# Choosing experts tile by tile and moving the overflow passes to the middle of each expert stage, in a four-layer transformer kernel

## What is computed

```python
lg = xt @ w_rg + b_rg                      # 4 group logits per token
g_sel = argmax(lg); p_grp = max(softmax(lg))
le_sel = (xt @ w_re + b_re).reshape(t, 4, 8)[g_sel]   # the 8 experts of that group
top_l, top_i = top_k(le_sel, 2)
gate = p_grp * softmax(top_l)
y = sum over the two chosen experts e: gate * ((silu(x @ w1[e]) * (x @ w3[e])) @ w2[e])
```

## Time and profile before

| | us |
|---|---|
| runs (3) | 1964.44, 1967.55, 1974.81; median 1967.55 |
| the profiled execution, its own time | 1970.61 |
| its span (first to last instruction) | 1968.9 |
| TensorE busy | 1561.1 (79%) |
| VectorE busy | 417.5 (21%) |
| ScalarE busy | 247.0 (13%) |
| weight queue's packets | 86.5% of 16 DMA engines' span |

### The profile page before, as it was taken

The page is one execution under the profiler, slowest core; times in us unless marked ns, Lnnn a source line. Parts: engine busy times, 40 slices in busy tenths (PEclk is TensorE's granted clock), DMA queues, the critical chain, the costliest instruction groups (busy, mean ns, idle before and its releaser), DMA issues.

```text
span 1968.9 us, 23180 instructions
## 1 busy us (share of the span) xinstructions
PE 1561.1 (79%) x10204; PEld 753.7 (38%) x10204; DVE 417.5 (21%) x900; ACT 247.0 (13%) x527; POOL 86.3 (4%) x140
## 2 busy tenths in 40 slices
PE   8898777899888787989996677776889777667675
PEld 4654433664464344445541222221355222212222
DVE  3341111226331110564410010000043000000001
ACT  1310000136211110156000000000011000000000
POOL 1100000101000000112100000000000000000000
PEclk9999988899899898999997888887899888888888
DMA  7659999669759999389689999999985999999995
GB/s 279 240 198 422 423 422 417 253 236 389 296 235 412 421 420 382 121 314 374 250 329 424 423 425 425 423 423 425 423 350 236 424 423 423 425 424 424 423 422 248
DMA packets 122894, 711.11 MB, mean 361 GB/s; under 512 B 8376, under 2 KB 13480, under 8 KB 49056
## 3 DMA queue, kind: packets, MB, share of 16 engines
q1 hardware_dynamic: 116368, 697.14, 86.5%
q0 software_dynamic: 4320, 9.78, 1.5%
q10 hardware_dynamic: 2096, 2.57, 0.4%
HBM read 708.17 MB, written 1.05 MB: 360 GB/s over the span
## 4 chain that ended last, share of the span: by engine, by line
PE 48%; DMA 39%; DVE 6%; SPq 2%; issue 2%; ACT 2%; POOL 0%; DVEq 0%; PEldq 0%; ACTq 0%; POOLq 0%
DMA ring<-in_moe_w 22%; PE pa L752 7%; PE pb L735 6%; DMA work<-in_moe_w 5%; DMA ring<-in_moe_w_down 5%; PE pa L770 4%; DMA work<-in_moe_w_down 3%; PE acc L814 3%; PE pb L720 3%; PE acc L1304 3%; PE acc L1309 3%; SPq L676 2%; PE acc L1049 2%; PE acc L1223 2%; DMA mod<-in_moe_w 2%
## 5 line engine op out<-in xcount | busy, mean ns | idle before, releaser
L735 PE MATMUL pb<-ring,XT 128*32 128x512 f32 x1488 | 278.9, 709 | 85.8 <-DMA ring<-in_moe_w 77.0
L752 PE MATMUL pa<-ring,work 128*32 128x512 f32 x1056 | 219.9, 754 | 79.1 <-DMA ring<-in_moe_w 46.2
L735 PEld LDWEIGHTS pb<-ring,XT 128*32 128x32 f32 x1488 | 64.6, 126 | 247.8 <-issue 122.5
L770 PE MATMUL pa<-work,HM 128*128 128x128 f32 x1024 | 131.6, 291 | 19.9 <-issue 19.9
L814 PE MATMUL acc<-XT,work 128*128 128x512 f32 x256 | 118.4, 605 | 35.2 <-DVE XT L870 22.4
L770 PEld LDWEIGHTS pa<-work,HM 128*128 128x128 f32 x1024 | 130.2, 207 | 34.8 <-issue 34.8
L860 DVE TENSOR_TENSOR work<-work,pb 128x256 f32<-128x256 f32 (+1 forms) x32 | 17.7, 555 | 574.0 <-PE pb L735 433.9
L735 PE MATMUL pb<-work,XT 128*32 128x512 f32 x480 | 114.5, 708 | 29.1 <-DMA work<-in_moe_w 29.1
L752 PEld LDWEIGHTS pa<-ring,work 128*32 128x32 f32 x1056 | 48.6, 132 | 203.6 <-issue 90.5
L720 PE MATMUL pb<-ring,XT 128*32 128x256 f32 x1728 | 109.8, 380 | 10.6 <-DMA ring<-in_moe_w_up 6.1
L752 PE MATMUL pa<-work 128*32 128x512 f32 x384 | 90.1, 784 | 26.0 <-DMA work<-in_moe_w 15.4
(11 more groups left out here) (403 smaller groups left out, 1741.3 us busy)
## 6 DMA issues: line engine op xcount, KB each, us to landing
ring<-in_moe_w SPq DMA_DIRECT2D x135, 2048.0 KB
work<-in_moe_w SPq DMA_DIRECT2D x46, 2048.0 KB
ring<-in_moe_w_up SPq DMA_DIRECT2D x28, 2048.0 KB
ring<-in_moe_w_gate SPq DMA_DIRECT2D x26, 2048.0 KB
ring<-in_moe_w_down SPq DMA_DIRECT2D x24, 2048.0 KB
ring<-in_w_mod SPq DMA_DIRECT2D x48, 1024.0 KB
mod<-in_moe_w SPq DMA_DIRECT2D x11, 2048.0 KB
work<-in_moe_w_down SPq DMA_DIRECT2D x8, 2048.0 KB
```

What stands on the lines that cost most here:

```text
L735: last = nc.tensor.matmul(hbank[m][j * CAP:(j + 1) * CAP, :], m_xg[:, k, j * CAP:(j + 1) * CAP], slot_of(s0 + j // 2)[:, at:at + fn], star ...
L752: last = nc.tensor.matmul(pa[j * CAP:(j + 1) * CAP, h, :], m_ht[:, c, j * CAP:(j + 1) * CAP], slot_of(i)[:, at:at + 512], start=(c == 0), ...
L770: last = nc.tensor.matmul(xg_ps[:, k, :], HM[:, tt, k * P:(k + 1) * P], m_p[:, tt, :], start=(tt == 0), stop=(tt == TT - 1))
```

## The change

- `PASS_AT = 4`: on all four engines the wait, the register loads and the branch around the overflow passes stand between rounds 3 and 4 and not between 6 and 7. The waits inside the condition are moved with it.
- The logits of tile t go to bank t of `pa`, and `logits_done` is raised once a tile. VectorE runs the choice once for each tile, in 16 operations of half the width; the match against the maximum and the order of the candidates are one operation, with the maximum read per partition. `order` is a new constant made by two operations on GpSimd. Both differences for the exponentials come behind `assign_ready`.
- In expert stages ScalarE copies all four turned halves.
- In the nsa phase 6 idle matmuls stand ahead of the transposes of tile 0 and 10 ahead of those of tile 1.

Context lines are mostly left out:

```diff
@@ -38,6 +38,7 @@
+PASS_AT = ROUNDS // 2
@@ -163,6 +164,7 @@
         iota = sb("iota", [P, CAP])
+        order = sb("order", [P, CAP])
@@ -298,15 +300,17 @@
             for t in range(TT):
+                if ph.kind == "nsa":
+                    warm_tensor(pe, (pa, pb)[t][:, 0, :], (6, 10)[t])
-        def transpose_scalar(act, n, dst):
-            for i in range(3):
+        def transpose_scalar(act, n, dst, parts=3):
+            for i in range(parts):
@@ -563,8 +567,8 @@
                 for k in range(KC):
-                    last = nc.tensor.matmul(pa[:, 0, t * 64:t * 64 + NG + NE], XT[:, k, t * P:(t + 1) * P], wr[:, k, :], start=(k == 0), stop=(k == KC - 1))
-            last.then_inc(logits_done, 1)
+                    last = nc.tensor.matmul(pa[:, t, 0:NG + NE], XT[:, k, t * P:(t + 1) * P], wr[:, k, :], start=(k == 0), stop=(k == KC - 1))
+                last.then_inc(logits_done, 1)
@@ -602,36 +606,37 @@
-            def first_of(out_, x, m, iv, tmp, n):
-                link(v.tensor_tensor(tmp, x, bc(m.unsqueeze(2), [P, TT, n]), ALU.is_equal))
-                link(v.scalar_tensor_tensor(tmp, tmp, -64.0, bc(iv.unsqueeze(1), [P, TT, n]), ALU.mult, ALU.add))
-                link(v.tensor_reduce(m_s[:, 15, :], tmp, AX.X, ALU.min))
-                link(v.tensor_tensor(out_, tmp, bc(m_s[:, 15, :].unsqueeze(2), [P, TT, n]), ALU.is_equal))
-            dve.wait_ge(logits_done, ph.moe + 1)
-            dve.wait_ge(wr_loaded, 96 * (ph.moe + 1))
-            link(v.tensor_tensor(m_log, pa[:, 0, 0:2 * 64].rearrange("p (t n) -> p t n", t=TT)[:, :, 0:NG + NE],
-                                 bc(br[:, :].unsqueeze(1), [P, TT, NG + NE]), ALU.add))
             gmax, l1, l2, dif = (m_s[:, i, :] for i in (0, 1, 2, 4))
-            link(v.tensor_reduce(gmax, lg, AX.X, ALU.max))
-            first_of(m_g[0], lg, gmax, iota[:, 0:NG], m_g[2], NG)
+            lm, o1, o2, tmp = m_t
+            def best(x, top, tmp, t, n):
+                at_ = m_s[:, 15, t:t + 1]
+                link(v.tensor_reduce(top[:, t:t + 1], x, AX.X, ALU.max))
+                link(v.scalar_tensor_tensor(tmp, x, top[:, t:t + 1], order[:, 0:n], ALU.is_equal, ALU.mult))
+                link(v.tensor_reduce(at_, tmp, AX.X, ALU.min))
+                return at_
+            dve.wait_ge(wr_loaded, 96 * (ph.moe + 1))
+            for t in range(TT):
+                dve.wait_ge(logits_done, TT * ph.moe + t + 1)
+                link(v.tensor_tensor(m_log[:, t, :], pa[:, t, 0:NG + NE], br[:, :], ALU.add))
+                g = m_g[2][:, t, :]
+                at_ = best(lg[:, t, :], gmax, g, t, NG)
+                link(v.tensor_scalar(g, g, at_, NEG, ALU.not_equal, ALU.mult))
+                link(v.tensor_tensor(lm[:, t, :].rearrange("p (g e) -> p g e", g=NG), le[:, t, :].rearrange("p (g e) -> p g e", g=NG),
+                                     bc(g.unsqueeze(2), [P, NG, EPG]), ALU.add))
+                at_ = best(lm[:, t, :], l1, tmp[:, t, :], t, NE)
+                link(v.tensor_scalar(o1[:, t, :], tmp[:, t, :], at_, None, ALU.is_equal))
+                link(v.scalar_tensor_tensor(lm[:, t, :], o1[:, t, :], 3 * NEG, lm[:, t, :], ALU.mult, ALU.add))
+                at_ = best(lm[:, t, :], l2, tmp[:, t, :], t, NE)
+                link(v.tensor_scalar(o2[:, t, :], tmp[:, t, :], at_, None, ALU.is_equal))
+                if t == 0:
+                    link(v.tensor_tensor(m_a[:, t, :], o1[:, t, :], o2[:, t, :], ALU.add))
+            v.tensor_tensor(m_a[:, t, :], o1[:, t, :], o2[:, t, :], ALU.add).then_inc(assign_ready, 1)
             v.tensor_tensor(m_g[1], lg, bc(gmax.unsqueeze(2), [P, TT, NG]), ALU.subtract).then_inc(rexp_in, 1)
-            link(v.tensor_scalar(m_g[2], m_g[0], 1.0, -NEG, ALU.subtract, ALU.mult))
-            lm, o1, o2, tmp = m_t
-            link(v.tensor_tensor(lm.rearrange("p t (g e) -> p t g e", g=NG), le.rearrange("p t (g e) -> p t g e", g=NG),
-                                 bc(m_g[2].unsqueeze(3), [P, TT, NG, EPG]), ALU.add))
-            link(v.tensor_reduce(l1, lm, AX.X, ALU.max))
-            first_of(o1, lm, l1, iota[:, 0:NE], tmp, NE)
-            link(v.scalar_tensor_tensor(lm, o1, 3 * NEG, lm, ALU.mult, ALU.add))
-            link(v.tensor_reduce(l2, lm, AX.X, ALU.max))
-            first_of(o2, lm, l2, iota[:, 0:NE], tmp, NE)
             v.tensor_tensor(dif, l2, l1, ALU.subtract).then_inc(rexp_in, 1)
-            v.tensor_tensor(m_a, o1, o2, ALU.add).then_inc(assign_ready, 1)
@@ -872,14 +877,14 @@
             n = moe_slots(ph.fn)
-            for g in range(ROUNDS - 1):
+            for g in range(PASS_AT):
             with sp.If(more > 0):
-                sp.wait_ge(freed, ph.slot0 + (ROUNDS - 1) * n)
+                sp.wait_ge(freed, ph.slot0 + PASS_AT * n)
@@ -890,7 +895,8 @@
             sp.wait_ge(xfreed, (base + more) * (ROUNDS * UNITS) + CREDIT)
-            whole_sync(sp, ph, ROUNDS - 1)
+            for g in range(PASS_AT, ROUNDS):
+                whole_sync(sp, ph, g)
@@ -908,7 +914,7 @@
-                pe.wait_ge(R[0]["y_copied"], 2 * (ROUNDS * (ph.moe + 1) - 1) + START)
+                pe.wait_ge(R[0]["y_copied"], 2 * (ROUNDS * ph.moe + PASS_AT) + START)
@@ -916,7 +922,8 @@
                         round_tensor(pe, ph, R[1], t, wait_full, (xfreed, unit), lambda i: ring[:, i % XSLOTS, :])
-            main_round(ROUNDS - 1)
+            for g in range(PASS_AT, ROUNDS):
+                main_round(g)
@@ -931,15 +938,15 @@
                      lambda e: e.wait_ge(freed, ph.slot0 + g * n + n))
-            for g in range(ROUNDS - 1):
+            for g in range(PASS_AT):
             with eng.If(more > 0):
-                eng.wait_ge(R[0]["added"], ROUNDS * (ph.moe + 1) - 1 + START)
-                eng.wait_ge(R[0]["rank_next"], ROUNDS * (ph.moe + 1) - 1 + START)
+                eng.wait_ge(R[0]["added"], ROUNDS * ph.moe + PASS_AT + START)
+                eng.wait_ge(R[0]["rank_next"], ROUNDS * ph.moe + PASS_AT + START)
@@ -973,6 +981,8 @@
             g.tensor_copy(iota[:, :], iota_i[:, :]).then_inc(consts, 1)
+            link(g.tensor_copy(order[:, :], iota_i[:, :]))
+            link(g.tensor_scalar(order[:, :], order[:, :], 64.0, None, ALU.subtract))
@@ -2361,7 +2371,7 @@
                         by_run_scalar(act, ph, 0)
-                    transpose_scalar(act, ph.xt, XT)
+                    transpose_scalar(act, ph.xt, XT, 4)
@@ -2378,7 +2388,6 @@
                 if ph.kind == "moe":
-                    transpose_vector(dve, ph.xt, XT)
```

## The result

The changed kernel takes 1943.36 us (median of 4 runs, 1941.98 to 1944.58), the kernel before 1966.04 beside it (4 runs, 1964.44 to 1974.81). The ratio is 0.9873, with a 95% interval of 0.9841 to 0.9905: faster by 1.3%, clear of the noise. The forecast was 1951.3 in a range of 1944 to 1961. The direction is right, the gain is larger than forecast, and the median lies just under the range. Profile against profile the gain is 26.0 us (1970.6 to 1944.58), where the sum made 16.3.

A forecast was written before the change was run, and what follows sets the result against it. Weight DMA was taken to bound expert stages, TensorE counting only at their beginnings and ends. 10.4 - 2.2 + 2.4 + 2.7 + 3.0 = 16.3 us off 1970.6 makes 1954.3, as a median 1951.3; range 1944 to 1961.

The forecast's parts named there:

- Stage 2's end: Round 7 of stage 2: without the overflow condition, idle gaps and slow passes go; gain 10.4 us.
- Stage 2's middle: Round 4 of stage 2: the moved stall frees slots late and the weight queue runs dry; cost 2.2 us.
- The other branch that the prediction named: Stage 2, round 4: if the second gap is absent, slots are freed before the queue is dry; cost 0.
- its upper bound of 7: Stage 2, round 4: if the stall is half as long again, 5.2 us more, the cost is about 7.
- Stage 1: Its end gains 2.4 us, then waits for round 7's last weights; the condition in its middle costs 0.
- VectorE's chain: Router, tile 1: 16 operations instead of 22 take 3.85 us; gain 2.7 us over four stages (0 to 4.2).
- The nsa phase's beginning: Idle matmuls keep the clock up for tile 1's transposes and L2116's first passes; gain 3.0 us (0 to 3.4).
- The clock may fall in another place of this stretch; I leave it at 0, with some 3 us either way.: Router: a shift of the clock's slow stretch was counted as 0, with some 3 us either way.
- The fourth copy: Router: ScalarE's copy of the fourth turned half ends when VectorE's did; cost 0, between -0.1 and 0.1 us.
- The stall did not stay at the end: Rival: round 7 is stopped again, only router and nsa gains remain, 5.7 us, 1961.9; chance 0.12.
- the gains were not clipped: Rival: stage 1's data, nsa weights or the router's clock take gains back, leaving 7.3 us, 1960.3; chance 0.14.
- the middle's stall did not empty the queue in any stage: Rival: round 4's stall empties the weight queue in every stage, 10.3 us slower, 1977.9; chance 0.05.

The follow-up runs named there:

- e7: The changed kernel without the overflow passes and their condition on all four engines; 1942.07 us (0.9861).
- e1: The kernel before with only the overflow condition moved between rounds 3 and 4; 1956.04 us (0.9923).
- e10: The kernel before with twelve idle matmuls under TensorE's wait for the first weights, shifting later code; 1965.0 us (0.9977).
- e11: The changed kernel with twelve idle matmuls under TensorE's wait for the first weights, shifting later code; 1945.33 us (0.9885).
- e6: The changed kernel with VectorE copying the fourth turned half again, as before the change; 1956.77 us (0.9958).
- e4: The changed kernel with the overflow condition back before the last round, router and nsa parts kept; 1950.44 us (0.9908).
- e3: The kernel before with only the idle matmuls ahead of the nsa phase's transposes; 1962.44 us (0.9959).
- e8: The kernel before without the overflow passes and their condition on all four engines; 1954.73 us (0.9919).
- e12: The kernel before with 12 instead of 6 idle matmuls ahead of TensorE's router wait in stages 2 and 3; 1959.28 us (0.9956).
- e2: The kernel before with only the router part: choice tile by tile, the constant and ScalarE's fourth copy; 1962.42 us (0.9960).
- e0: The changed kernel a second time, nothing altered; 1943.0 us (0.9867).
- e9: The changed kernel with six additions linked into tile 1's VectorE chain, making it as long as before; 1955.62 us (0.9936).

## Why the prediction was right and wrong

- **Stage 2's end** (-10.4): right, -10.30; the last weights fit, as worked out, and e7 without any condition has -10.34. The "40.3 us after the old L814 began" run from the down weights of round 6 (L752 at 744.52), not from L814 (750.54); the time worked out from them is not changed by it.
- **Stage 2's middle** (+2.2): +0.68, and 0.01 in rounds 3 to 6, where the stall is. The other branch that the prediction named came true: the second gap is absent in round 4, so the slots are freed before the queue is dry, or nearly. e1 shows what it would have been with two gaps, +4.47, between the forecast's 2.2 and its upper bound of 7. The time given to a stall that differs with the layout of the code was a coin toss. The working itself gives 2.1, and the sum took 2.2. By the Trainium skill (Runtime: NRT & Kernel Launch, Instruction fetch mechanics) a taken branch out of the current page, a block of instructions, forces a fetch. The traces agree, with a packet of the instruction queue in each of the 56 gaps, and e10 and e11 agree that the second gap is a matter of where the code lies. Where a block ends in the code no run here shows.
- **Stage 1** (-2.4, middle 0): right, -2.61 and +0.13. The new wait for the last down weights is there.
- **VectorE's chain** (3.85 us; -2.7 in four routers): the chain is right, 3.79. The four stretches came out at -3.08, but partly by luck: stages 1 to 4 were given 0.2, 1.15, 1.15 and 0.2 and measured 0.41, 1.12, 0.41 and 1.14. In stage 3 the shorter chain leaves TensorE no wait, but its carry (L591) takes 3.60 us where it took 1.96 (L587), with a granted clock of 0.82 for 0.91 in the 19 us around; stage 4 made up for it.
- **The nsa phase's beginning** (-3.0): right, -3.08. It doesn't always come: in the eight kernels with these idle passes the same stretch is 1.07 (e6) to 3.18 us (e4) shorter. In e3, at -2.08, the transposes are shorter, but the first passes of the projection still take 3.68, where in e4 and e7 they take 1.99. What decides stays open.
- **The step that failed** is the sentence "The clock may fall in another place of this stretch; I leave it at 0, with some 3 us either way." The term was put at nothing as if the clock could fall either way, but here it has a direction. Over all fourteen profiled kernels, stage 2's stretch from ranking to round 0's addition takes 22.15 to 22.51 us in the seven where TensorE's wait ahead of the ranking is at most 0.83 us, and 25.22 to 25.34 in six of the seven where it is 1.88 or more (23.70 in the seventh, e1). In stage 3 the same split holds (34.02 to 35.25 us up to 0.83, 35.76 to 38.33 from 1.88 on), in stage 4 with one exception, and in stage 1 there is none: e8 has a wait of 1.89 us there and the same 20.24 us behind it. So a wait of this length is often followed by the lower level, and not always. e12 shows it for the wait alone, with the chain unchanged. The term is -2.84 in stage 2 and -1.87 in stage 3, -4.97 in all, and larger than the shorter chain itself. The rows for it were at hand: the prediction used waits of about a microsecond "that left the clock up" for stage 1's end and for the nsa phase, and by its own sum the router's wait goes from 1.89 to 0.74; it did not put the two together.
- **Two stretches that the sum did not hold.** The end of the nsa phase gave 1.58 us. Behind the same wait of 1.99 us it takes 46.1 us in six of the fourteen kernels (before, e2, e3, e8, e11, e12), 44.5 in the changed kernel and e0, and 41.9 in e1, e6, e7 and e9 (43.9 in e4 and 46.7 in e10), though none changes its code. The same passes behind the wait take 1.47 or 0.85 us there, so the clock is at work too, but nothing in the experiments says what decides. Stage 4's last round gave 2.73. It was -2.64 in e0 and -2.70 in e4, whose condition is at the end, and -0.51 in e1, whose condition is in the middle: it isn't the position. With a wait of 1.36 us for the last weights the last passes take 3.63 us, with 2.54 they took 5.09; why these weights are in about a microsecond earlier was not found out.
- **The fourth copy** (0): right as a swap, wrong as a part. The prediction costed its duration, and gave tile 0's chain "about 1.2 us to spare" without saying that this spare time hangs on the copy leaving VectorE. e6 puts 11.4 us on it.
- **The rivals.** The stall did not stay at the end, the gains were not clipped (the sum given for that case, 7.3, should be 9.7 by its own terms, 10.4 - 2.2 + 1.5, which makes 1957.9), and in the changed kernel the middle's stall did not empty the queue in any stage: e7 and e0 differ by 0.9 us. The Trainium skill's 51 to 108 ns for a branch (Advanced Engine Details and Errata, Control Flow Timing) don't describe what was seen here: the stops measured 2.4 to 5.25 us each, and e8, which takes the condition out, is 14.4 us faster.

The parts don't add as they look. The three alone give 28.1 us against 26.1 for the whole (e0), but e2 and e3 count 6.7 and 5.0 us at stage 2's end, where one of the two gaps and the slow passes around it are gone, which e10 brings about as well, with idle matmuls under the first wait, and e1 counts the 4.2 us of the nsa phase's end. Part of what this change measures against the kernel before is that kernel's unlucky layout: each of the five other kernels with the condition at the end has one gap there.

## What to carry to other kernels

A branch around a large block that is never run belongs where a queue of loads has something in hand, in the middle of a stage that is bound by weights, not ahead of its last round: here it cost 14.4 us at the end, with two stops in stage 2, and under 1 in the middle, and moving it gave 7.4 us where each stage had one stop. When a wait of TensorE is shortened or filled, look at the durations of the instructions behind it in both profiles, not only at the wait: in stage 2, what followed a wait of 1.88 us or more was 2.7 us or more longer than behind one of 0.83 or less, in all kernels but one. And before a part is credited with a gain, shift the code with nothing else changed: a second stop and the slow passes around it, 5 us in all, may come or go by that.

## What was not expected of the hardware

- Useless work is worth time. Six more idle matmuls (12 passes) in a wait raised the granted clock from 0.84 to 1.00 over 14 us and gave 3.2 us (e12, stage 2).
- The stop behind a condition is 3.6 to 4.5 us in most places (2.4 to 5.25 in all), and in some layouts the same gather stops a second time, for 2.3 to 3.1 us. In each stop lies a 16 KB packet of the instruction queue, and TensorE goes on 1.2 to 1.9 us after it has landed. An edit far from it made round 7 of stage 2 shorter by 5.0 to 5.4 us in e3, e10 and e12.
- An operation on VectorE that reads one value per partition takes 0.25 us at 128 by 32, its neighbours 0.19; at 128 by 4 it is 0.22 and 0.16.
- The clock's stretches fall differently in kernels whose code there is the same: 41.9, 44.5 or 46.1 us for the end of the nsa phase.
